# The order of the last prompt preparation steps and the first prompt attention steps, in a two-layer attention and gMLP trunk

## The reference

```python
q = (rms_norm(q_lat, g_q_lora) @ w_q_up).reshape(B, S, N_HEADS, QK_HEAD)      # 8 heads of 64 + 32
q = concat([rms_norm(q_nope, g_qn), apply_rope(rms_norm(q_rope, g_qr))])
kv = (ckv_all @ w_kv_up).reshape(B, T, N_HEADS, QK_NOPE + V_HEAD)
k = concat([rms_norm(k_nope, g_kn), broadcast(k_rope)]);  v = the other 64 columns of each head
s = einsum('bqhe,bkhe->bhqk', q, k) * QK_HEAD ** -0.5, masked block-causally in chunks of 64
o = softmax(s) @ v
x = x + concat([rms_norm(o), rms_norm(gmlp)]) @ w_o;   x = x + swiglu(rms_norm(x))
```

## Time and profile before

| | |
|---|---|
| median of three executions | 1410.85 us (1410.61 to 1413.23) |
| the profiled execution | 1417.39 us, of it the span from the first to the last instruction 1415.6 us |
| busy share of the span, PE / DVE / ACT / POOL | 96% / 64% / 42% / 61% |
| mean granted TensorE clock, share of full speed | 0.981 |
| stretch of the change, layer 0 and layer 1 | about 193 to 215 us, about 886 to 908 us |

### The profile page before, as it was taken

The page is one execution under the profiler, slowest core; times in us unless marked ns, Lnnn a source line. Parts: engine busy times, 40 slices in busy tenths (PEclk is TensorE's granted clock), DMA queues, the critical chain, the costliest instruction groups (busy, mean ns, idle before and its releaser), DMA issues.

```text
span 1415.6 us, 25340 instructions
## 1 busy us (share of the span) xinstructions
PE 1352.3 (96%) x9448; PEld 1247.7 (88%) x9448; DVE 912.7 (64%) x1490; ACT 599.5 (42%) x953; POOL 866.3 (61%) x460
## 2 busy tenths in 40 slices
PE   6999989998999999999999989889899999999998
PEld 6885657898999999999998756779899999999997
DVE  3456467487666766676736475665866766666665
ACT  4336467444333333333342365764443333333331
POOL 3645057286777777777655443464777777777771
PEclk8999999999999999999999999999999999999999
DMA  7110021131322222222421000221232222222221
GB/s 229 60 38 11 5 61 30 32 89 54 96 90 89 89 89 89 89 89 89 130 89 52 26 5 1 60 60 31 60 90 90 89 89 89 89 89 89 89 89 68
DMA packets 138577, 102.35 MB, mean 72 GB/s; under 512 B 8972, under 2 KB 125136, under 8 KB 138512
## 3 DMA queue, kind: packets, MB, share of 16 engines
q1 hardware_dynamic: 135848, 100.46, 23.6%
q10 hardware_dynamic: 2664, 1.02, 0.3%
HBM read 98.10 MB, written 3.36 MB: 72 GB/s over the span
## 4 chain that ended last, share of the span: by engine, by line
PE 83%; DVE 9%; ACT 2%; issue 2%; POOL 2%; DMA 1%; ACTq 0%; SPq 0%; DVEq 0%
PE ps L2199 33%; PE ps L1907 9%; PE ps L1911 9%; PE ps L1908 9%; PE ps L1852 4%; PE ps L1890 3%; PE ps L1891 3%; PE ps L1892 3%; PE ps L2140 2%; PE ps L2120 2%; POOL rs L754 2%; PE ps L2004 2%; PE ps L2010 1%; DVE hs_lo L1312 1%; PE ps L2097 1%
## 5 line engine op out<-in xcount | busy, mean ns | idle before, releaser
L754 POOL TENSOR_TENSOR rs<-ms,mhalf 128x8 f32<-128x8 f32 (+5 forms) x66 | 139.7, 2120 | 200.8 <-DVE ms L1442 80.5
L853 POOL TENSOR_TENSOR w_lo<-raw,w_hi 128x1024 fp32r<-128x1024 f32 x132 | 229.9, 1769 | 42.4 <-ACT w_hi L1263 39.7
L1677 DVE TENSOR_REDUCE raw<-raw 128x512 f32<-128x1024 f32 x184 | 230.6, 1254 | 0.5
L853 POOL TENSOR_TENSOR w_lo_a<-raw,w_hi_a 128x512 fp32r<-128x512 f32 x88 | 179.5, 2052 | 69.8 <-ACT w_hi_a L1263 69.8
L1907 PE MATMUL ps<-act_hi,w_hi 128*128 128x288 f32 x704 | 195.9, 293 | 3.5 <-issue 3.5
L1908 PE MATMUL ps<-act_lo,w_hi 128*128 128x288 f32 x704 | 196.1, 294 | 0.0
L1639 DVE TENSOR_TENSOR xT<-ps,xT 128x576 f32<-128x576 f32 x192 | 142.3, 751 | 46.3 <-PE ps L1911 46.2
L2199 PE MATMUL ps<-t_hi,w_hi 128*128 128x288 f32 x528 | 157.4, 298 | 7.4 <-DVE side L1702 6.1
L2199 PE MATMUL ps<-t_lo,w_hi 128*128 128x288 f32 x528 | 156.8, 297 | 0.0
L2199 PE MATMUL ps<-t_hi,w_lo 128*128 128x288 f32 x528 | 156.5, 296 | 0.0
L1911 PE MATMUL ps<-act_hi,w_lo 128*128 128x288 f32 x704 | 150.5, 295 | 0.0
(11 more groups left out here) (239 smaller groups left out, 3496.9 us busy)
## 6 DMA issues: line engine op xcount, KB each, us to landing
raw<-in_w_gate SPq DMA_DIRECT2D x88, 256.0 KB, 3.7
raw<-in_w_up SPq DMA_DIRECT2D x88, 256.0 KB, 3.6
raw<-in_w_down SPq DMA_DIRECT2D x20, 1024.0 KB, 4.9
raw<-in_w_in SPq DMA_DIRECT2D x10, 1024.0 KB, 5.5
raw<-in_w_o SPq DMA_DIRECT2D x16, 512.0 KB, 5.3
x_tm<-in_x_prompt SPq DMA_DIRECT2D x4, 512.0 KB, 5.2
raw<-in_w_down SPq DMA_DIRECT2D x8, 256.0 KB, 3.5
out_y_prompt<-x_tm SPq DMA_DIRECT2D x8, 256.0 KB, 2.2
```

The costliest lines, as they stand in the source:

```text
L754: pool.tensor_tensor(rs[:, c:c + n], ms[:, c:c + n], mhalf[:, 0:n], ALU.pow).then_inc(rs_ready, 1)
L853: pool.tensor_tensor(lo[:, k, cols], src, hi[:, k, cols].bitcast(F32), ALU.subtract).then_inc(lo_split, 1)
L1677: dve.tensor_reduce(raw[:, 2, j * Q:(j + 1) * Q], added(a, b), AX.X, ALU.add).then_inc(sums_added, 1)
```

## The change

The steps of PE keep their work and get another order: attention step 0 now stands ahead of preparation step 6, step 1 ahead of step 7, step 2 ahead of step 8 and step 3 ahead of step 9. On DVE and ACT attention step 0 moves ahead of preparation step 7, step 1 ahead of step 8, step 2 ahead of step 9.

```diff
-P_ORDER = PREP[2:7] + [ATTEND[0], PREP[7], ATTEND[1], PREP[8], ATTEND[2], PREP[9]] + ATTEND[3:]
-P_ORDER_READERS = PREP[2:7] + [PREP[7], ATTEND[0], PREP[8], ATTEND[1], PREP[9], ATTEND[2]] + ATTEND[3:]
-assert P_ORDER[-len(P_STEPS) - 1] == ("prep", len(P_TILES) + 1)
+P_ORDER = PREP[2:6] + [ATTEND[0], PREP[6], ATTEND[1], PREP[7], ATTEND[2], PREP[8], ATTEND[3], PREP[9]] + ATTEND[4:]
+P_ORDER_READERS = PREP[2:7] + [ATTEND[0], PREP[7], ATTEND[1], PREP[8], ATTEND[2], PREP[9]] + ATTEND[3:]
+assert P_ORDER_READERS[-len(P_STEPS) - 1] == ("prep", len(P_TILES) + 1)
```

## The result

The changed kernel has a median of 1434.08 us over 14 executions (1417.45 to 1454.63); the kernel before, over 14 beside them, 1413.11 us (1407.22 to 1422.70). It is slower. The ratio is 1.0103, with an interval from 1.0076 to 1.0130. By the ratio the loss is 14.6 us, by the medians 21.0. The profiled execution took 1446.10 us, span 1444.3 us.

A forecast was written before the change was run, and what follows sets the result against it. TensorE, busy 96% of the span, was taken as the bound. Per layer 2.64 lag + 0.9 clock - 0.66 head = 2.88 us, twice 5.8, on 1410.85: 1416.6 us; forecast 1414 to 1420 (0.70), full range 1411.5 to 1420.5.

The forecast's parts named there:

- The path: Scores of step 0 to value product 1, counted step by step at full clock: value product 1 at 215.71, against 213.07.
- The lag: Value product 1 of attention step 1 starts 2.64 us later per layer, and the rest of the attention with it.
- The waits themselves: TensorE waits 4.1 us inside K3's projection, 2.07 ahead of K2's transposes and 1.3 ahead of value product 1.
- The head of the output projection: Its first product needs two low parts from VectorE, not three: wait 1.8 us for 2.45, 0.66 us gained.
- The sum: Per layer 2.64 + 0.9 - 0.66 = 2.88 us, over two layers 5.8 us, giving 1416.6 us.
- The clock: Slow stretches brought by the gaps of 4.1 and 2.07 us cost 0.9 us a layer, at most 2.2.
- more is lost: Rival: clock at its upper bound, old path without its own slow stretch in timed runs; 1422.0 us, chance 0.10.
- The signs that the prediction named: In the changed timeline: TensorE's waits of 4.1, 2.07 and 1.3 us, shifted masks, 1.8 us at the output projection's head.
- its last sign: Prediction is wrong if TensorE's stretches at 1.2 GHz change in number by more than one a layer.
- the clock gives it back: Rival: no new slow stretches in the attention, output projection's head keeps full clock; 0.6 us, 1411.4 us, chance 0.09.
- The banks don't bind: Rival: TensorE does not wait for exponentials to free banks, leaving 0.2 us of lag; 1409.9 us, chance 0.05.
- Absorbed: Rival: VectorE sets the attention's pace, so the 2.64 us vanish and the head's gain stays; 1406.1 us, chance 0.06.

The follow-up runs named there:

- experiment 3: Changed kernel with the keys' half of K3's projection made five times and the scores of attention step 4 twice; median 1425.42 us, ratio 1.0081 to the kernel before.
- experiment 1: Changed kernel timed again with no edit; median 1430.87 us, ratio 1.0140 to the kernel before.
- experiment 5: Changed kernel with only the scores of attention step 4 made twice; median 1418.96 us, ratio 1.0032 to the kernel before.
- experiment 2: Changed kernel with the keys' half of K3's projection made five times instead of once; median 1431.04 us, ratio 1.0129 to the kernel before.
- experiment 6: Changed kernel with one place of the ring of banks left out ahead of value product 1; median 1421.70 us, ratio 1.0059 to the kernel before.
- experiment 7: Kernel before with VectorE taking the row extremes of attention step 0 three times; median 1415.23 us, ratio 1.0026 to the unedited kernel before.
- experiment 9: Kernel before with VectorE taking the row extremes of attention step 3 seven times; median 1429.89 us over 12 executions, ratio 0.9995 from the four below 1428 us.
- experiment 12: Changed kernel with the scores of attention steps 4, 15 and 17 made twice; median 1411.63 us, ratio 0.9995 to the kernel before.
- experiment 10: Kernel before with the scores of attention steps 15 and 17 made twice; median 1407.46 us, ratio 0.9962 to the unedited kernel before.
- experiment 4: Kernel before with the new order of VectorE and ScalarE alone, TensorE and banks unaltered; median 1424.14 us, ratio 1.0067 to the kernel before.
- experiment 11: Kernel before with the scores of attention steps 15 and 17 made twice and of step 1 three times; median 1403.38 us, ratio 0.9936.

## Why the prediction was wrong

The direction was right, the size was not: 5.8 us forecast, 21 us measured between medians and 14.6 by the ratio, outside the range either way.

**The path: right.** With the scores of step 0 laid on each other (192.63 measured, 194.01 in the working), the exponentials of step 0 came at 201.4 (forecast 201.7), those of step 1 at 206.8 (206.9), the transposes of K2 at 208.5 (208.5), value product 1 at 215.7 (215.7). The lag is 2.67 us a layer (forecast 2.64). The waits themselves measured 3.53 us where 4.1 was forecast, about half of that because the exponentials of step 0 came 0.3 sooner, and 0.54 where it was 2.07: the work ahead of it ran at half clock from 202.6 to 206.0. There that stretch cost at most 0.3 us, as it mostly took up slack in front of the exponentials of step 1: from the transposes of Q2 to value product 1 it is 22.5 us where the clock is full throughout (experiment 3, both layers) and 22.4 to 22.8 with the stretch (the changed kernel and experiment 1; 23.6 in layer 0 of experiment 5, where it was 6.8 us long). The slack was used up, though: the copy of Q3 on ACT ends at 205.46, when the exponentials of step 1 begin, and not 0.4 us ahead.

**The head of the output projection: right in the wait, short in the gain.** The wait is 1.79 for 2.45 us, 0.66 less as counted. The half clock behind it was gone as well in the profile after (1.00 from 278.1 on). The sum put that at nothing; it is worth 1.5 us a layer (from its first product to the next turned outputs 3.25 us in place of 4.79). It is no accident of one profile: in the 14 layers profiled in which this wait is 1.8 us none has a slow stretch behind it, of the 14 in which it is 2.45 us 11 have.

**"The clock": the step that failed.** The prediction gave it 0.9 us a layer, at most 2.2, all of it for the two larger waits. Six layers were profiled with the wait of 1.3 us ahead of value product 1 (the changed kernel and experiments 1 and 2). In four of them the clock cost 16 to 18 us behind this wait, 17.9 in each layer of the first profile, and in the other two nothing. Two things in that step were wrong. It took the length of a slow stretch, "over 3 us", from the earlier trace rows for all places, though one of these stands among the preparation steps and the other in the output projection, and none where attention steps alone follow. (The trace of the kernel before has one there too, behind the wait at step 13, and it is no longer than the others; a stretch of 40 us is nowhere in it.) And it gave its bounds to the two larger waits and none to the smallest, 1.3 us, although value product 1 behind it opens the attention steps. Experiments 2, 5 and 6 put the loss on that wait; 7 and 9 show that it is not the length of a wait that decides, and that a small wait at the opening of the attention steps does the same in the kernel before, in one of its two profiled layers. Rival "more is lost" named the right cause with the wrong price.

The signs that the prediction named were no help. All its waits came, one of them shorter, and its last sign, that slow stretches change in number by more than one a layer, did not: there are three a layer before and two after. Their length is what changed, from 10 to 48 us a layer.

The rival "the clock gives it back" is out as the outcome, but its arithmetic held in the one layer of the unaltered changed kernel that was profiled without the long stretch: in layer 0 of experiment 1 the part from the transposes of Q2 to the turned outputs behind the head of the output projection takes 71.49 us, before 71.25, and the rival had 0.3 us more a layer. "The banks don't bind" is out: all three waits ended with exponentials, and with another bank the smallest went (experiment 6). "Absorbed" too: in experiment 12 value product 1 is 2.7 to 2.8 us late, and the part from there to the end of the attention is no shorter than in experiment 10 (40.3 us in both).

What stays open: why the clock falls behind the wait of 1.3 us in some layers and not in others; what in the work behind it keeps the clock down for 41 to 44 us; what sets the length of a slow stretch behind the wait at step 13 (about 3.4 us in nine of the layers profiled, 10 to 21 us in six, none in two), and with it the 0.67% of experiment 4.

## What to carry to other kernels

A wait of TensorE has two prices: its length, and what the clock does to the work behind it. The second depends on the place: a wait of 3.5 us inside K3's projection cost 0 to 1.1 us by the clock, one of 1.3 us at the opening of the attention steps up to 18 us. So before a bank or an order is chosen, count each new wait, the small ones too, and look at what long run of work without a wait follows it. If a wait cannot be removed, put repeated products into it: the scores of three steps made once or twice more took 0.6% off the time of the kernel before.

## What the runs showed of the hardware

In the attention steps PE was busy for 44.00 of 44 us by the profile and its clock still stayed at 1.2 GHz. The 1.81 us of the value product at 217.02, 1.00 before, say the same as the granted clock. Being busy by the profile is not enough to get the clock back. Five layers show such a stretch of 41 to 44 us, two of the changed kernel and one each of experiments 1, 2 and 9; in all five it ended among the steps of the last query tile, whose scores are 512 columns wide. The same steps ran at full clock in other layers (41.1 us for 59.0), and the clock came back after 3.4 us among transposes and small products elsewhere (the rows of experiment 3), so the kind of products alone does not explain it. The Trainium skill, "TensorE: Matmul & The Clock Gate", Part 1, has activity release the slow clock; the trace agrees for the short stretches, and differs for these 44 us.

Whether a wait of one length brings the clock down differs from layer to layer in one execution (experiments 1, 2 and 7), and the kernel's times spread with it: 1417 to 1460 us for the changed kernel, experiment 1 included, at mean clocks from 0.984 to 0.951, and 1401.65 to 1407.07 us for that of experiment 11.
